# Three raw weight slots in place of four, and five half chunks of split weights in place of four, in a one-layer diffusion backbone

## The reference

```python
mod_l = (jax.nn.silu(c) @ w_ada + b_ada)[:, None, :]        # 2048 x 12288, also for c_ctx
ul = (xl * (1 + sc1_l) + sh1_l) @ w_in                      # 2048 x 13824
uc = (xc * (1 + sc1_c) + sh1_c) @ w_in
ya_c, ya_l = _hgrn_mixer(uc, ul, ...)                       # gated linear recurrence
yc_c, yc_l = _attention_mixer(uc, ul, attn_sink, need_ctx)
yb_l = _pool_mixer(ul, pool_w, pool_scale)
xl = _layer_norm(ALPHA * xl + g1_l * _merge_branches(ul, (ya_l, yb_l, yc_l), w_branch, w_out), ln1_g, ln1_b)
xl = _layer_norm(ALPHA * xl + g2_l * _sq_relu_mlp(xl * (1 + sc2_l) + sh2_l, w_ff1, w_ff2), ln2_g, ln2_b)
```

## Time and profile before

| | |
|---|---|
| median of 3 runs | 2043.79 us (2041.5 to 2047.46) |
| profiled execution, its own time | 2049.65 us |
| span of the profile | 2047.9 us |
| mean granted PE clock | 0.966 |
| busy: PE, DVE, ACT, POOL | 1913.1, 1266.0, 779.4, 436.9 us |
| moved by DMA | 409.03 MB, 200 GB/s on average |

### The profile page before, as it was taken

The page is one execution under the profiler, slowest core; times in us unless marked ns, Lnnn a source line. Parts: engine busy times, 40 slices in busy tenths (PEclk is TensorE's granted clock), DMA queues, the critical chain, the costliest instruction groups (busy, mean ns, idle before and its releaser), DMA issues.

```text
span 2047.9 us, 26151 instructions
## 1 busy us (share of the span) xinstructions
PE 1913.1 (93%) x10808; PEld 1641.7 (80%) x10808; DVE 1266.0 (62%) x1420; ACT 779.4 (38%) x886; POOL 436.9 (21%) x335
## 2 busy tenths in 40 slices
PE   5888899999898989999999999699999999999996
PEld 1467787889888867777778887698899899889975
DVE  1245546686656576667867666865466557546675
ACT  1121223445445455544334443333333333333332
POOL 0000000002736342022421000452035005303500
PEclk7898999999999989999999999799999999999998
DMA  9865554455333343446556675365665656556642
GB/s 401 322 270 197 213 198 164 165 195 176 124 104 119 108 142 136 165 164 265 228 214 260 256 258 185 117 234 205 215 241 223 203 209 220 213 187 225 227 167 80
DMA packets 58743, 409.03 MB, mean 200 GB/s; under 512 B 6272, under 2 KB 8960, under 8 KB 9728
## 3 DMA queue, kind: packets, MB, share of 16 engines
q1 hardware_dynamic: 54144, 394.29, 52.7%
q10 hardware_dynamic: 4480, 13.07, 1.7%
HBM read 405.24 MB, written 2.10 MB: 199 GB/s over the span
## 4 chain that ended last, share of the span: by engine, by line
PE 71%; DVE 13%; DMA 4%; DVEq 4%; issue 3%; POOL 3%; ACT 2%; POOLq 0%; ACTq 0%
PE main L1241 12%; PE main L1242 12%; PE main L1243 12%; PE main L1201 9%; PE main L1202 9%; PE main L1203 9%; DVE asum L824 5%; DVE wlo L803 3%; DMA raw<-in_w_in 2%; DVEq L823 2%; DMA raw<-in_w_ada 2%; PE side L1259 1%; PE side L1417 1%; ACT whi L381 1%; PE main L1278 1%
## 5 line engine op out<-in xcount | busy, mean ns | idle before, releaser
L803 DVE TENSOR_TENSOR wlo<-raw,whi 128x1024 fp32r<-128x1024 f32 x552 | 724.9, 1339 | 444.6 <-ACT whi L381 444.1
L381 ACT CAST whi<-raw 128x1024 fp32r<-128x1024 f32 x552 | 571.7, 1050 | 864.6 <-PE main L1243 358.5
L1201 PE MATMUL main<-h,whi 128*128 128x256 f32 x1024 | 291.4, 285 | 8.2 <-DVE h L1109 5.5
L1202 PE MATMUL main<-h,whi 128*128 128x256 f32 x1024 | 290.9, 284 | 0.0
L1203 PE MATMUL main<-h,wlo 128*128 128x256 f32 x1024 | 290.8, 284 | 0.0
L1201 PE MATMUL main<-hCL,whi 128*128 128x256 f32 (+1 forms) x800 | 264.3, 330 | 4.3 <-DVE ya L985 2.2
L1202 PE MATMUL main<-hCL,whi 128*128 128x256 f32 (+1 forms) x800 | 260.5, 326 | 0.0
L1203 PE MATMUL main<-hCL,wlo 128*128 128x256 f32 (+1 forms) x800 | 260.3, 325 | 0.0
L824 DVE SCALAR_TENSOR_TENSOR asum<-raw,sm,asum 128x512 f32<-128x512 f32 x240 | 200.9, 837 | 19.7 <-issue 0.9
L1241 PE MATMUL main<-whi,hid 128*128 128x512 f32 x512 | 201.1, 393 | 4.1 <-issue 2.7
L1201 PEld LDWEIGHTS main<-h,whi 128*128 128x128 f32 x1024 | 197.8, 193 | 8.9 <-DVE h L1109 5.9
(11 more groups left out here) (228 smaller groups left out, 2696.9 us busy)
## 6 DMA issues: line engine op xcount, KB each, us to landing
raw<-in_w_f SPq DMA_DIRECT2D x128, 1024.0 KB, 5.0
raw<-in_w_in SPq DMA_DIRECT2D x108, 1024.0 KB, 5.0
raw<-in_w_ada SPq DMA_DIRECT2D x96, 1024.0 KB, 6.9
raw<-in_w_br SPq DMA_DIRECT2D x24, 1024.0 KB, 6.9
raw<-in_w_out SPq DMA_DIRECT2D x16, 1024.0 KB, 4.9
xin<-in_xT SPq DMA_DIRECT2D x4, 1024.0 KB, 9.9
ax<-in_xtok ACTq DMA_DIRECT2D x1, 2048.0 KB, 7.9
lng<-in_rows ACTq DMA_DIRECT2D x2, 1024.0 KB, 4.9
```

Of the source, the lines that this page charges most:

```text
L381: nc.scalar.copy(whi[:, q % 4], raw[:, slot, 2 * h:2 * h + 2]).then_inc(hi_made, 1)
L803: TT(wlo[:, q % 4], raw[:, slot, 2 * h:2 * h + 2], whi[:, q % 4].bitcast(F32), ALU.subtract).then_inc(lo_made, 1)
L1201: mm(out, w_hi, x_hi, start=start, stop=False)
L1202: mm(out, w_hi, x_lo, start=False, stop=False)
```

## The change

`RAW` becomes 3 and a new constant `HALVES` = 5 replaces the four half chunks of the split ring. The memory is the same: 4 x 8 KB + 2 x 4 x 4 KB before, 3 x 8 KB + 2 x 5 x 4 KB after, 64 KB a partition each time. The order of the chunks and the order of the instructions on each engine stay; which chunk a transfer or a split waits for changes, and the kernel's lines after the first constants move down by one.

```diff
-RAW = 4
+RAW = 3
+HALVES = 5
@@ build
         raw = at("raw", [P, RAW, CK, PW], 0)
-        whi = at("whi", [P, 4, 2, PW], 32 * KB, F32R)
-        wlo = at("wlo", [P, 4, 2, PW], 48 * KB, F32R)
+        whi = at("whi", [P, HALVES, 2, PW], 24 * KB, F32R)
+        wlo = at("wlo", [P, HALVES, 2, PW], 44 * KB, F32R)
@@ scalar: split
-                    if q >= 4:
-                        which, count = PN.last[q - 4]
+                    if q >= HALVES:
+                        which, count = PN.last[q - HALVES]
                         act.wait_ge(ended[which], count)
-                    nc.scalar.copy(whi[:, q % 4], raw[:, slot, 2 * h:2 * h + 2]).then_inc(hi_made, 1)
+                    nc.scalar.copy(whi[:, q % HALVES], raw[:, slot, 2 * h:2 * h + 2]).then_inc(hi_made, 1)
@@ vector: split
-                    TT(wlo[:, q % 4], raw[:, slot, 2 * h:2 * h + 2], whi[:, q % 4].bitcast(F32),
+                    TT(wlo[:, q % HALVES], raw[:, slot, 2 * h:2 * h + 2], whi[:, q % HALVES].bitcast(F32),
                        ALU.subtract).then_inc(lo_made, 1)
@@ tensor: half_ready
-                return q % 4
+                return q % HALVES
```

## The result

The changed kernel took 2125.81 us (median of four runs, 2120.09 to 2127.53) against 2042.85 for the kernel before on the same chip (2041.5 to 2047.46): 1.0391 times, with a 95% interval of 1.0365 to 1.0418. It is slower, as forecast, but by 83 us and not by 43. The time lies above the range of 2056 to 2112.

The account below looks back on a forecast made before the run. PE was taken as busy throughout, but "vals" as bound by a chain through the split chunk's transfer, ACT and DVE. Terms 3 + 17 + 24.5 + 13 - 14 = +43.5 on 2049.65 gave 2093, median 2087; range 2056 to 2112.

Parts of the forecast that it names:

- Start and ada stage, +3: Term for the first stage: three delays of 2.5 us less about 4.5, so +3, bounds 0 to 7.5.
- The three places: Ada stage: +2.5 us each at the start and at two places where PE stalls for a split chunk.
- the 4.5 us taken off for an earlier split: Ada stage: first sums stand behind a split that waits for PE, now half a chunk less, about 4.5 us gained.
- "vals", +17: Split chunk issued second at a sum's end lands after 7.5 us, not 5.0; seven turns x 2.45, bounds 12 and 21.
- The rival of the double buffer: Landing has slack in "vals" and "forget", three slots are ample, the extra half chunk wins: 2022 to 2029, chance 0.04.
- "forget", +24.5: Turns become 11.7 us: +21 over three later groups, +3.5 for PE's clock after longer stalls; bounds 12 and 32.
- The rival in which little of it arrives: Only "vals" grows: about 8 of 24.5 us arrive in "forget", "gates" stays with PE; median 2058, chance 0.14.
- "gates", +13: Groups with sums: +0.5 each for four, +3 each for three with POOL at work, +2 on entry; bounds 0 and 22.
- The last link: End of the slot chain in a "gates" group, from q1's landing through its split to the next sum's end.
- The gains, -14: Fifth half chunk shortens PE's waits for low parts and a column (14.8 us), clock dips could add 5; bounds -5 and -22.
- The wait for the column: Attention: PE waits 3.0 us behind a column DVE makes late; predicted gone or under 1 us.
- The MLP and "mix", 0: MLP: 20.3 us chain hidden under PE's 23.0, so 0; "mix": neither ring shortens PE's waits, 0, from -4 to +4.

Follow-up runs that it names:

- e: The changed kernel with a fourth raw slot in the ada stage alone (its first 36 chunks): 2117.23 us, 1.0360 of the kernel before.
- b: The changed kernel with the next split chunk of "vals" fetched ahead of the two sum chunks, as DVE uses them: 2079.48 us, 1.0172 of the kernel before.
- f: The changed kernel with chunks fetched in DVE's order of use in "forget" alone: 2100.85 us, 1.0281 of the kernel before.
- g: The changed kernel with chunks fetched in DVE's order of use in "gates" alone: 2100.54 us, 1.0280 of the kernel before.
- d: The kernel before (four slots, four half chunks) with fetches in DVE's order of use in every stage with sum chunks: 2015.72 us, 0.9859 of the kernel before.
- d2: The same kernel as d, timed again: 2015.12 us, 0.9849 of the kernel before.
- h2: Second timing of the changed kernel with order of use in all four stages and a fourth slot in the ada stage: 2010.76 us, 0.9827 of before.

## Why the prediction was wrong in size and right in kind

The sum missed by 32.4 us of trace time (75.9 against 43.5): ada 6.4, "vals" 3.7, "forget" 3.1, "mix" 1.7, "gates" 8.3, the gains 7.9, the end 1.3. Every one has the same sign. The difference of medians, 83, is 7 more again, because the profiled execution before stood that much above its median.

**Start and ada stage, +3: a credit that did not come.** The three places were right in kind and size. PE starts 2.6 us late on the start's work (6.4 late at 43 us, but it then has chunks in hand and makes some of it up), 2.4 more at the place of the earlier trace rows, 2.8 more at the second, 7.8 in all against 7.5. At the place of the earlier trace rows four chunks ran through; now the fourth waits:

```profile
76.73 1.93 PE L1260 MATMUL side<-raw,sR 128*32 128x512 f32 x8 [3.29 <-DMA raw<-in_w_ada]
...
124.62 1.07 PE L1260 MATMUL side<-raw,sR 128*32 128x512 f32 x8 [2.45 <-DMA raw<-in_w_ada]
```

The second row is a place that I had not counted, and from there on PE is 1.5 later. In all, PE waits for raw chunks in this stage, before and after:

```profile
PE side L1259 <- DMA raw<-in_w_ada: 8.9, 6, 3.3
```
```profile
PE side L1260 <- DMA raw<-in_w_ada: 21.1, 9, 3.5
```

With the fourth slot of e it is 7.7 us. The step that failed is the 4.5 us taken off for an earlier split: nothing of it came. ACT's split stands in its list behind four copies that wait for PE's finished block, and five halves do not change that:

```profile
143.56 0.59 ACT L434 COPY vc<-main 128x512 f32<-128x512 f32 x1 [3.80 <-PE main L1281]
...
147.64 0.59 ACT L434 COPY vl<-main 128x512 f32<-128x512 f32 x1 [0.77 <-PE main L1281]
148.12 2.00 ACT L382 CAST whi<-raw 128x1024 fp32r<-128x1024 f32 x2
```

In the trace before it stands behind the same four copies with the same waits, 9.41 us earlier. I had asked what the split waits for, and not what stands ahead of it on its engine.

**"vals", +17: right, a little small.** Place, pair and chain are as predicted. The second of the pair landed after 7.15, 6.88, 7.35, 8.93, 8.63, 7.13 and 7.45 us, 7.6 on average and not 7.1, which is the 0.5 us between turns of 18.0 and 17.5. The rival of the double buffer failed here. The advice of the Trainium skill, "Trainium Kernel Development and Optimization" (Best Practices), to double-buffer is borne out only with the order of b beside it: three slots gave a turn of 18.0 us in one order of fetch and full overlap in the other.

**"forget", +24.5: right.** Turns of 11.9 for 11.7; the three later groups came 7.6, 9.3 and 9.0 us late, where I had 7.0 and 1.2 for the clock. The rival in which little of it arrives falls with the 25.0 us of PE's waits. f shows that the order, by which a split chunk waits for the slot of the sum just ended, was the cause.

**"gates", +13: mechanism right, terms too small.** The first sum of the stage ends 53.3 us late, as late as the stage began, so the +2 on entry did not come. The three groups with POOL took 38.3 on average (964.68 to 1079.53) and not 37.6: 11.4 more than before, against +9. The rest is 9.9 us, where I had 2 for the late groups: the group at 1079.53 took 47.9 us for 45.9, three more took 35.3 each, and 1.7 us came behind the last sum. Before, those three took 33.3 on average, not the 34.0 of the one that I had read. After, then before:

```profile
1127.45 0.33 SPq L366 DMA_DIRECT2D raw<-in_w_ada  x1
```
```profile
1060.66 0.33 SPq L365 DMA_DIRECT2D raw<-in_w_in  x1
```

Three groups further on the issues stand at 1233.39 and at 1160.48: 105.9 us after, 99.8 before. The chain was right as far as the landing of q1, 27.5 us in the forecast: it came 27.5 us after 964.68 and 27.7 after 1127.45. The last link was too short. It took 11.3 us at 1003.44, where the forecast with POOL has 10.1, and 7.3 to 7.9 in the late groups for 6.8. There POOL still works for 1.3 us beside DVE's pair of low parts, which takes 3.47 us and not 2.4:

```profile
1156.27 3.47 DVE L804 TENSOR_TENSOR wlo<-raw,whi 128x1024 fp32r<-128x1024 f32 x2 [0.22 <-ACT whi L382]
```

The chain has two sums and three pairs of low parts, and the 37.6 lengthen one of each without saying why. It came near because POOL works little outside the last link (in the group shown from 991.65 to 1002.86), which was not foreseen. The term stays inside its bounds, 0 to 22. g shows that the order caused all of it.

**The gains, -14: the step that failed most beside ada.** Only 6 us came in the traces, all in attention, and not all of those are steady (d against d2). I had counted PE's waits for low parts in "gates" as waits for the split ring. They were waits for DVE or its weights: with four or five halves there are sixteen of them in the order of the change, 22.8 and 22.1 us, and six, 8.5 us, in the order of use. The 2.7 us at the start of the MLP stayed also. The wait for the column fell from 3.0 only to 2.1, where I had expected under 1. The wait for `pr`, 2.4 us, which the forecast does not name, went.

**The MLP and "mix", 0: right for the MLP.** The MLP's window is full, and its fourth slot was not missed. "mix" added 1.7, inside its bounds of -4 to +4.

What stays open: why the ada stage came 9.4, 8.4 and 15.0 us late in kernels with the same code in it (after, g, f); what decides whether the clock falls behind a short wait in attention; and what four slots with five halves would do in the old order, which was not run, nor was a ring of its own for each kind of chunk.

## What to carry to other kernels

In a ring that several kinds of work share, a transfer starts when the use that frees its slot ends, and not before those written ahead of it have been issued. So write the order of fetch as the order of use, and only then count slots: here that was worth 100 us with three slots (2125.81 to 2025.73) and 29 with four, where the whole change of slots cost 83. A longer ring pays only where a free place in it is the last thing waited for: before counting a wait as its gain, look at what stands ahead of the work in its engine's list and at when its data came. And a gain of a few us in one trace wants a second trace of the same kernel.

## What the runs showed of the hardware

Of two transfers of 1 MB issued 0.37 us apart, the second landed 6.8 to 8.9 us after its issue, where one by itself took 4.7 to 5.2. A sum instruction on DVE took 1.40 to 1.63 us with POOL at work and 0.75 without, in the same group of "gates". PE's mean granted clock was lower the more it waited: 0.949 in the kernel after, 0.966 before, 0.976 in h2, for the same 10808 matmuls. Behind one and the same wait of 2.4 us the granted clock over 20 us was 0.91 in one execution and 1.00 in another.
